# The opening stage of a hybrid GLA and pooling block: modulation columns, folds and early products by eighths of the features in place of quarters

## The chip, the cores and the metric

The kernel runs on one core of a Trainium2 chip. The metric is the device time of one execution in microseconds (us), the median over several runs. The core has five engines with instruction queues of their own: TensorE (PE, with its weight loads shown apart as PEld), VectorE (DVE), ScalarE (ACT), GpSimd (POOL) and SyncE (SP). SP issues nearly all DMAs here. Sixteen DMA engines move the bytes. Engines order themselves by semaphores, written out by hand in this kernel.

## The reference

One inference step of one transformer-like block, for 128 prompt tokens and 512 sample tokens (640 in all) of width 2048. What matters here is its beginning:

```python
xp = layer_norm(x_prompt, ln_in_g, ln_in_b)              # xs alike
mod_ctx = silu(c_ctx) @ w_ada + b_ada                    # 2048 x 12288; mod_lat alike from c
sh1, sc1, g1, sh2, sc2, g2 = split(mod, 6)
h = x * (1 + sc1) + sh1                                  # per feature, one pair for each token group
z = h @ w_in                                             # 33 units of 128 output columns
...                                                      # GLA scans, pooling, w_out, layer norm
gate, up = split(h2 @ w_gu, 2)                           # h2 = x * (1 + sc2) + sh2
y = layer_norm(ALPHA * x + g2 * ((silu(gate) * up) @ w_down))
```

All of it is float32. The kernel splits each operand of the big products into a high part and a rest and adds three products (high x high, high x rest, rest x high).

## The kernel before, in words

The features (2048) lie on the partitions in 16 blocks of 128, numbered k; the 640 tokens are the free dimension, in two halves of 320. Before any product of `w_in` can run on a block k, that block of h must be there, and for it the scale and shift of its 128 features: two sections of 2048 columns of `w_ada`, 33.5 MB in all. This opening stage, the prologue, does the following.

- **Loads.** SP issues, in one order written by hand: two small tables, the five token tiles of x (1 MB each), the steps of `w_ada`, and between them the first `w_in` units (1 MB each). `load_first` loads step i: 512 rows of the contraction by 512 columns, 1 MB in rows of 2 KB. `FIRST_SLOT` names its buffer; a buffer is loaded again once the step that used it before has been multiplied (`first_used`). Buffer 9 is the first half of `raw_w` and waits for three finished weight splits. `UNIT_AFTER` says after which step a unit is loaded; `load_unit(u)` for u of 2 or more waits until `split_done` reaches u - 1.
- **Input layer norm.** DVE takes the moments of an x tile, ACT its root and the normalisation, PE turns it (`turn_x`), DVE and ACT copy the result out to `xT`. PE's queue has these turns between the first four steps.
- **Modulation.** `ada_step` multiplies one step: four column groups of the array at once. Four steps fill one bank with a row of 512 columns (scale: bank 6, shift: bank 7). ACT copies the row out (`first_row`), PE turns it into columns and sums the groups (`first_cols`), DVE adds the bias (`add_bias`). Each quarter of the features needs eight steps, four for the scale and four for the shift.
- **Fold and split.** DVE folds the gain and bias of the layer norm into scale and shift (`fold_norm`, four small instructions in a chain). ACT applies them to a block of `xT` (two instructions, for the two token groups), DVE casts the high part and subtracts for the rest (`split_tile`, semaphore `h_split`). Blocks alternate between two temporary buffers. Weight units are split likewise (`split_in` on ACT, `split_rest` on DVE).
- **Early products.** The first three units (`EARLY`) are multiplied piece by piece while modulation is still running: `main_part(n, b)` is unit n by the four blocks of quarter b, 24 matmuls. They stand in PE's queue behind steps 2, 5 and 7 of the next quarter. After step 31 the last quarter of all three units follows.
- **Afterwards.** ACT copies unit 0 out (`evac(0)`), then splits unit 3, whose buffer unit 0 has left (`split_in(3)`, wait on `unit_used`), DVE makes its rest, and PE starts unit 3. From here a schedule of 33 units, `w_out`, the FFN and the down product follows; SP's next loads wait for the 16th block and then for `unit_used` of 3, and POOL's first work behind its first memset waits for the 16th block too.

PE runs its queue strictly in order: a wait in front of an early product holds the steps behind it.

Of the kernel before, what the change touches and what calls it, by code (L numbers as in the profile page):

```python
# [166 lines left out]
FIRST_STEPS = 32  # L167
# [158 lines left out]
def backbone(nc, x_all, state_gla, w_ada, w_in_b, wa2, w_pool_l, w_out, w_gu_b, w_down, consts,  # L326
# [91 lines left out]

    def first_slot(i):

        if i < 8:
            at = 2 * D + STEP * i
            return x_raw[:, at:at + STEP].rearrange("p (k c) -> p k c", k=4)
        src = lo(S_X, STEP) if i == 8 else raw_w[:, 0, :]
        return src.rearrange("p (k c) -> p k c", k=4)
# [9 lines left out]
    FIRST_USES = [[i for i in range(FIRST_STEPS) if FIRST_SLOT[i] == n] for n in range(N_FIRST)]  # L435
# [83 lines left out]
    first_in = [sem(f"first_in{i}") for i in range(N_FIRST)]  # L519
# [139 lines left out]
    def _(sp):  # L659
# [46 lines left out]
        sp.wait_ge(first_used, FIRST_USES[9][-1] + 1)  # L706
# [258 lines left out]
    def _(act):  # L965
# [295 lines left out]
        act.wait_ge(folded, 5)  # L1261
# [108 lines left out]
    def _(dve):  # L1370
# [42 lines left out]
        def add_bias(i, q, dst, src, done):  # L1413

            bias = b_ada_col[:, i, 4 * q:4 * q + 4].unsqueeze(2).to_broadcast([P, 4, 2])
# [31 lines left out]
        for q in range(4):  # L1447
            for g in range(2):
                i = 2 * q + g
                section = SECTIONS[g][1]  # L1450
                if i == 3:
                    split_rest(2)
                dve.wait_ge(mod_turned, i + 1)
                add_bias(section, q, mod_col[:, section, 4 * q:4 * q + 4, :],
                         ps[:, 6 + g, 0:8].rearrange("p (k c) -> p k c", c=2), mod_cols)
            dve.wait_ge(mod_cols, 2 * q + 2)
            fold_norm(V_LNIN, 4 * q, 4)
            if q == 0:
                split_rest(0)
            for k in range(4 * q, 4 * q + 4):  # L1460
                dve.wait_ge(h_tmp, k + 1)
                split_tile(high[:, PRO_TMP + (k % 2) * T:PRO_TMP + (k % 2) * T + T], k, h_split)
            if q == 0:
                split_rest(1)
# [53 lines left out]
        for kind, a, b, uses in SCHEDULE:  # L1518
# [3 lines left out]
            elif kind == "adacol":  # L1522
# [5 lines left out]
                add_bias(2 + slot, q, mod_col[:, slot, 4 * q:4 * q + 4, :],  # L1528
# [234 lines left out]
        dve.wait_ge(folded, 5)  # L1763
# [261 lines left out]
    def _(pe):  # L2025
# [21 lines left out]
        def main_part(n, b):  # L2047

            part = KG_ORDER[b] if n == N_IN - 1 else b
            for half in range(2):  # L2050
                for k in range(4 * part, 4 * part + 4):
# [19 lines left out]
        def first_cols(i):  # L2071
# [3 lines left out]
            for k in range(4):  # L2075
# [5 lines left out]
        used = [0] * N_FIRST  # L2081
        for i in range(FIRST_STEPS):
            n = FIRST_SLOT[i]
            used[n] += 1
            q, m = i // 8, i % 4
            pe.wait_ge(first_in[n], 16 * used[n])
# [391 lines left out]
```

## Time and profile before

| | us |
|---|---|
| three runs | 2706.84, 2711.62, 2713.73 |
| median | 2711.62 |
| profiled execution, its own time | 2708.05 |
| profiled execution, span of the trace | 2706.2 |

| engine | busy us | share of the span |
|---|---|---|
| PE | 2637.0 | 97% |
| PEld | 2352.4 | 87% |
| DVE | 1443.2 | 53% |
| ACT | 897.4 | 33% |
| POOL | 639.6 | 24% |

The page divides the span into 40 slices of 67.7 us. PE is busy for 5 tenths in the first slice and for 9 or more in all others up to the last (7). Modulation and the early products lie in the first two slices. All times within the trace are counted from the start of the span.

### The profile page before, as it was taken

What the parts mean: (1) busy time and instruction counts of PE and PEld (TensorE: products, weight loads), DVE (VectorE), ACT (ScalarE), POOL (GpSimd) and SP (SyncE); (2) the same over time, 40 slices, a digit from 0 to 9 for tenths busy, and PEclk for the clock granted to TensorE, in tenths of its full rate; (3) what the DMA queues carried; (4) which work ended last, traced back from release to release, by engine and by line L of the source; (5) the groups of instructions that cost most, each with busy time, mean ns of one, the idle gap of its engine ahead of it and who ended that gap; (6) DMA issues with size and microseconds to landing.
All of it is one profiled execution on the core that took longest, in us unless ns stands there. A gap on an engine that the chain in (4) does not pass through costs nothing.

```text
span 2706.2 us, 37404 instructions
## 1 busy us (share of the span) xinstructions
PE 2637.0 (97%) x16040; PEld 2352.4 (87%) x16040; DVE 1443.2 (53%) x1681; ACT 897.4 (33%) x940; POOL 639.6 (24%) x217
## 2 busy tenths in 40 slices
PE   5999999999999999999999999999999999999997
PEld 3687878797988879999999999999999888888875
DVE  5323332346575458666555545555556444454578
ACT  4333333332311154333333333333333333333343
POOL 0000000000000001434443444344433333333440
PEclk8999999999999999999999999999999999999999
DMA  9775757422463142332233323322334645464576
GB/s 373 285 268 208 275 202 273 158 90 87 181 219 118 63 161 81 109 108 89 92 108 109 94 87 109 109 92 89 109 109 152 242 173 211 173 212 166 207 245 238
DMA packets 179384, 438.11 MB, mean 162 GB/s; under 512 B 9980, under 2 KB 25732, under 8 KB 173076
## 3 DMA queue, kind: packets, MB, share of 16 engines
q1 hardware_dynamic: 176916, 430.48, 46.0%
q10 hardware_dynamic: 2304, 5.24, 0.5%
q8 instruction: 127, 2.08, 0.3%
q14 instruction: 37, 0.30, 0.0%
HBM read 401.83 MB, written 33.85 MB: 161 GB/s over the span
## 4 chain that ended last, share of the span: by engine, by line
PE 79%; DVE 6%; DMA 5%; POOL 4%; ACT 2%; issue 2%; SPq 1%; POOLq 0%; ACTq 0%; DVEq 0%
PE ps L2310 10%; PE ps L2311 10%; PE ps L2312 10%; PE ps L2387 6%; PE ps L2389 6%; PE ps L2388 6%; PE ps L2063 5%; PE ps L2065 5%; PE ps L2064 5%; PE ps L2257 3%; PE ps L2043 3%; PE ps L2259 3%; PE ps L2258 3%; DMA raw_w<-w_gu_b 2%; PE ps L2104 2%
## 5 line engine op out<-in xcount | busy, mean ns | idle before, releaser
L1670 DVE TENSOR_TENSOR w_lo<-raw_w,w_hi 128x1024 fp32r<-128x1024 f32 x264 | 348.2, 1320 | 299.8 <-ACT w_hi L1214 297.5
L1214 ACT ACTIVATE w_hi<-raw_w 128x1024 fp32r<-128x1024 f32 x264 | 270.2, 1054 | 610.5 <-POOL raw_w L954 370.5
L2310 PE MATMUL ps<-x_hi,w_hi 128*128 128x320 f32 x1408 | 436.2, 310 | 2.1 <-DVE x_lo L1750 1.4
L2312 PE MATMUL ps<-x_hi,w_lo 128*128 128x320 f32 x1408 | 435.1, 309 | 0.0
L2311 PE MATMUL ps<-x_lo,w_hi 128*128 128x320 f32 x1408 | 435.0, 309 | 0.0
L1805 DVE TENSOR_TENSOR x_lo<-low,x_hi 128x2560 fp32r<-128x2560 f32 (+2 forms) x55 | 223.6, 4065 | 261.3 <-ACT x_hi L1307 261.3
L945 POOL TENSOR_TENSOR low<-raw_w 128x1024 f32<-128x1024 f32 x41 | 101.2, 2469 | 1094.6 <-DMA raw_w<-w_gu_b 1027.5
L2387 PE MATMUL ps<-w_hi,x_hi 128*128 128x512 f32 x880 | 343.1, 390 | 3.3 <-DVE w_lo L1965 1.9
L2389 PE MATMUL ps<-w_hi,x_lo 128*128 128x512 f32 x880 | 342.4, 389 | 0.0
L2388 PE MATMUL ps<-w_lo,x_hi 128*128 128x512 f32 x880 | 342.4, 389 | 0.0
L2310 PE MATMUL ps<-low_r,w_hi 128*128 128x320 f32 x1072 | 332.0, 310 | 2.3 <-DVE w_lo L1670 1.5
L2312 PE MATMUL ps<-low_r,w_lo 128*128 128x320 f32 x1072 | 331.2, 309 | 0.0
L2311 PE MATMUL ps<-low_r,w_hi 128*128 128x320 f32 x1072 | 331.2, 309 | 0.0
L2063 PE MATMUL ps<-x_hi,w_hi 128*128 128x320 f32 x1024 | 324.4, 317 | 6.6 <-ACT low L1109 4.8
L2065 PE MATMUL ps<-x_hi,w_lo 128*128 128x320 f32 x1024 | 317.8, 310 | 0.0
L2064 PE MATMUL ps<-x_lo,w_hi 128*128 128x320 f32 x1024 | 317.7, 310 | 0.0
L960 POOL TENSOR_TENSOR w_lo<-raw_w,w_hi 128x2048 fp32r<-128x2048 f32 x44 | 203.9, 4633 | 355.5 <-ACT w_hi L1316 355.5
L2310 PEld LDWEIGHTS ps<-x_hi,w_hi 128*128 128x128 f32 x1408 | 264.3, 188 | 3.4 <-issue 1.6
L2311 PEld LDWEIGHTS ps<-x_lo,w_hi 128*128 128x128 f32 x1408 | 264.3, 188 | 0.0
L2312 PEld LDWEIGHTS ps<-x_hi,w_lo 128*128 128x128 f32 x1408 | 264.3, 188 | 0.0
L1381 DVE TENSOR_TENSOR w_lo<-raw_w,w_hi 128x2048 fp32r<-128x2048 f32 x48 | 110.0, 2291 | 259.0 <-ACT w_hi L981 258.8
L1316 ACT ACTIVATE w_hi<-raw_w 128x2048 fp32r<-128x2048 f32 x55 | 105.4, 1917 | 378.8 <-PE ps L2389 360.9
(239 smaller groups left out, 4358.0 us busy)
## 6 DMA issues: line engine op xcount, KB each, us to landing
raw_w<-w_gu_b SPq DMA_DIRECT2D x180, 512.0 KB, 5.7
low<-w_ada SPq DMA_DIRECT2D x68, 1024.0 KB, 6.9
raw_w<-w_down SPq DMA_DIRECT2D x55, 1024.0 KB, 5.1
low<-hidden_scratch SPq DMA_DIRECT2D x33, 1280.0 KB, 6.0
raw_w<-w_in_b SPq DMA_DIRECT2D x33, 1024.0 KB, 9.1
x_raw<-w_ada SPq DMA_DIRECT2D x25, 1024.0 KB, 15.4
raw_w<-w_out SPq DMA_DIRECT2D x16, 1024.0 KB, 5.2
hidden_scratch<-high SPq DMA_DIRECT2D x44, 320.0 KB, 5.9
```

The source lines that it names most:

```text
L1214: nc.scalar.activation(weight(0, w), src, ACT.Copy).then_inc(prod_hi, 1)
L1670: nc.vector.tensor_tensor(weight(1, n), src, weight(0, n).bitcast(F32), ALU.subtract).then_inc(prod_split, 1)
L1805: nc.vector.tensor_tensor(hid_slot(x_lo, j), hid_raw(j), hid_slot(x_hi, j).bitcast(F32), ALU.subtract).then_inc(hid_split, 1)
L2063: mm(out, wh, xh, start=first, stop=False)
L2064: mm(out, wh, xl, start=False, stop=False)
L2065: ins = mm(out, wl, xh, start=False, stop=last)
L2310: mm(out, wh, version(v, 0, k), start=first and k == 0, stop=False)
L2311: mm(out, wh, version(v, 1, k), start=False, stop=False)
L2312: ins = mm(out, wl, version(v, 0, k), start=False, stop=last and k == HK - 1)
L2387: mm(ps[:, (i + 7) % 8, :], xh, rh, start=begin, stop=False)
L2388: mm(ps[:, (i + 7) % 8, :], xh, rl, start=False, stop=False)
L2389: ins = mm(ps[:, (i + 7) % 8, :], xl, rh, start=False, stop=end)
```

## The change

A step becomes half as wide: 256 columns, 512 KB in rows of 1 KB, so 64 steps in place of 32. Eight steps now serve an eighth of the features, two blocks. Columns, bias, fold, ACT's affine pass, split and early products all go by two blocks (`early_part`, 12 matmuls). Each 1 MB buffer holds two steps; two more buffers are opened in blocks 0 to 6 of `xT`, free once seven blocks are split. Steps now count on 16 semaphores of their own, and step i is issued only once step i - 16 has been multiplied. `EARLY_PARTS` gives for each unit which eighths are multiplied behind steps 2, 5 and 7 of which eighth. ACT and DVE split weight units 0, 1 and 2 after the blocks of eighths 0, 1 and 2; before, they split unit 0 ahead of the blocks, unit 1 after the first quarter and unit 2 in the second. Unit 4 is loaded once step 63 has been multiplied.

```diff
-FIRST_STEPS = 32
+FIRST_STEPS = 64
...
-UNIT_AFTER = {7: 0, 8: 1, 11: 2, 31: 3}
+UNIT_AFTER = {7: 0, 11: 1, 15: 2, 63: 3}
...
-FIRST_SLOT = (0, 1, 2, 3, 4, 5, 6, 7, 0, 1, 2, 5, 6, 7, 8, 0, 1, 2, 9, 6, 7, 8, 1, 6, 2, 9, 7, 8, 2, 9, 7, 8)
-N_FIRST = 10
+FIRST_SLOT = (0, 1, 2, 3, 4, 5, 6, 7, 0, 1, 2, 5, 6, 7, 8, 0, 1, 2, 9, 6, 7, 8, 2, 9, 7, 8, 2, 9, 10, 11, 8, 9)
+N_FIRST = 12
+FIRST_IN_FLIGHT = 16
+EIGHTHS = 8
+EARLY_PARTS = ({e: (e - 1,) for e in range(1, 8)},
+               {2: (0, 1), 3: (2,), 4: (3,), 5: (4,), 6: (5,), 7: (6,)},
+               {3: (0, 1), 4: (2, 3), 5: (4,), 6: (5,), 7: (6,)})
...
+    def first_place(i):
+
+        return 2 * FIRST_SLOT[i // 2] + i % 2
...
         def load_first(i):
 
-            n = FIRST_SLOT[i]
+            n = first_place(i)
             before = [j for j in FIRST_USES[n] if j < i]
+            if i >= FIRST_IN_FLIGHT:
+                sp.wait_ge(first_used, i - FIRST_IN_FLIGHT + 1)
             if before:
                 sp.wait_ge(first_used, before[-1] + 1)
-            elif n == 8:
+            elif n // 2 == 8:
                 sp.wait_ge(turned, 4)
-            elif n == 9:
+            elif n // 2 == 9:
                 sp.wait_ge(split_done, 3)
-            group, part = SECTIONS[i // 4 % 2][0], i // 8
-            sp.dma_start(first_slot(n), w_ada_v[group, part, i % 4]).then_inc(first_in[n], 16)
+            elif n // 2 > 9:
+                sp.wait_ge(h_split, 7)
+            group, e = SECTIONS[i // 4 % 2][0], i // 8
+            c = 256 * (e % 2)
+            sp.dma_start(first_slot(i), w_ada_v[group, e // 2, i % 4][:, :, c:c + 256]
+                         ).then_inc(first_in[i % FIRST_IN_FLIGHT], 16)
...
-        sp.wait_ge(first_used, FIRST_USES[9][-1] + 1)
+        sp.wait_ge(first_used, max(FIRST_USES[18] + FIRST_USES[19]) + 1)
         load_unit(4, w_in_b[4])
...
-            nc.scalar.activation(high[:, at:at + 512], ps[:, 6 + i % 2, :], ACT.Copy).then_inc(mod_rows, 1)
+            nc.scalar.activation(high[:, at:at + 256], ps[:, 6 + i % 2, 0:256], ACT.Copy).then_inc(mod_rows, 1)
...
-        first_row(0)
-        first_row(1)
-        split_in(0)
-        for q in range(4):
-            if q:
-                first_row(2 * q)
-                if q == 1:
-                    split_in(2)
-                first_row(2 * q + 1)
-            for k in range(4 * q, 4 * q + 4):
+        for e in range(EIGHTHS):
+            first_row(2 * e)
+            first_row(2 * e + 1)
+            for k in range(2 * e, 2 * e + 2):
                 tmp = high[:, PRO_TMP + (k % 2) * T:PRO_TMP + (k % 2) * T + T]
-                if k % 4 == 0:
-                    act.wait_ge(folded, k // 4 + 1)
+                if k % 2 == 0:
+                    act.wait_ge(folded, e + 1)
...
-            if q == 0:
-                split_in(1)
+            if e < EARLY:
+                split_in(e)
...
-        for q in range(4):
+        for e in range(EIGHTHS):
...
+                dve.wait_ge(mod_turned, 2 * e + g + 1)
+                add_bias(section, 2 * e, 2, mod_col[:, section, 2 * e:2 * e + 2, :],
+                         ps[:, 6 + g, 0:4].rearrange("p (k c) -> p k c", c=2), mod_cols)
+            dve.wait_ge(mod_cols, 2 * e + 2)
+            fold_norm(V_LNIN, 2 * e, 2)
+            for k in range(2 * e, 2 * e + 2):
                 dve.wait_ge(h_tmp, k + 1)
                 split_tile(high[:, PRO_TMP + (k % 2) * T:PRO_TMP + (k % 2) * T + T], k, h_split)
-            if q == 0:
-                split_rest(1)
+            if e < EARLY:
+                split_rest(e)
...
-            for k in range(4):
+            for k in range(2):
                 c = PRO_ROW + 512 * (i % 2) + k * P
...
+        def early_part(n, e):
+
+            for half in range(2):
+                for k in range(2 * e, 2 * e + 2):
...
+                    if half == 0:
+                        pe.wait_ge(h_split, k + 1)
+                    mm(out, wh, xh, start=k == 0, stop=False)
+                    mm(out, wh, xl, start=False, stop=False)
+                    ins = mm(out, wl, xh, start=False, stop=k == KT - 1)
+            if e == EIGHTHS - 1:
+                ins.then_inc(unit_used, 1)
...
             if i % 8 == 4:
                 first_cols(i // 4 - 1)
             elif i % 8 == 7:
                 first_cols(i // 4)
-            if q and i % 8 in (2, 5, 7):
+            if i % 8 in (2, 5, 7):
                 u = (2, 5, 7).index(i % 8)
-                pe.wait_ge(split_done, u + 1)
-                main_part(u, q - 1)
+                for part in EARLY_PARTS[u].get(e, ()):
+                    pe.wait_ge(split_done, u + 1)
+                    early_part(u, part)
         for u in range(EARLY):
-            main_part(u, 3)
+            early_part(u, EIGHTHS - 1)
```

## Rows read from the trace of the kernel before

**Rows 1.** The page, its span.

```profile
span 2706.2 us, 37404 instructions
```

**Rows 2.** Windows of 10 us: busy us of PE, PEld, DVE, ACT, POOL, then PEclk, DMA share, GB/s.

```profile
50.00:60.00 10.00, 6.68 (x27) 3.29 (x28) 6.14 (x8) 4.20 (x5) 0.00 (x0) 0.50 1.04 395
...
80.00:90.00 10.00, 9.65 (x74) 6.54 (x67) 1.83 (x4) 0.90 (x2) 0.00 (x0) 1.00 1.03 371
...
120.00:130.00 10.00, 8.24 (x52) 7.24 (x51) 5.09 (x8) 5.66 (x10) 1.10 (x3) 1.00 0.00 0
130.00:140.00 10.00, 10.00 (x70) 10.00 (x69) 4.58 (x2) 3.83 (x6) 0.00 (x0) 1.00 0.39 129
```

**Rows 3.** Timeline of PE at the end of the prologue: start us, duration us, instruction.

```profile
114.29 1.06 PE L2043 MATMUL ps<-x_raw,perm 128*32 128x512 f32 x8
115.17 1.04 PE L2043 MATMUL ps<-low,perm 128*32 128x512 f32 x8
116.93 1.05 PE L2077 MATMUL ps<-perm,high 128*128 128x2 f32 x8 [0.72 <-ACT high L1006]
117.85 0.40 PE L2063 MATMUL ps<-x_hi,low_r 128*128 128x320 f32 x1
...
121.56 0.42 PE L2063 MATMUL ps<-x_hi,w_hi 128*128 128x320 f32 x1
...
122.83 0.41 PE L2063 MATMUL ps<-x_hi,w_hi 128*128 128x320 f32 x1 [0.54 <-DVE x_lo L1438]
...
134.79 0.31 PE L2063 MATMUL ps<-x_hi,w_hi 128*128 128x320 f32 x1
```

**Rows 4.** Timeline of DVE at the end of the prologue.

```profile
120.68 0.83 DVE L1438 TENSOR_TENSOR x_lo<-high,x_hi 128x640 fp32r<-128x640 f32 x1
...
121.94 0.83 DVE L1438 TENSOR_TENSOR x_lo<-high,x_hi 128x640 fp32r<-128x640 f32 x1
...
130.53 2.29 DVE L1381 TENSOR_TENSOR w_lo<-raw_w,w_hi 128x2048 fp32r<-128x2048 f32 x1 [5.14 <-ACT w_hi L981]
```

**Rows 5.** Timeline of ACT at the end of the prologue.

```profile
116.28 0.60 ACT L1006 ACTIVATE high<-ps 128x512 f32<-128x512 f32 x1 [8.63 <-PE ps L2043]
...
120.41 0.80 ACT L1038 ACTIVATE high<-low,perm 128x512 f32<-128x512 f32 x1
...
127.95 0.75 ACT L1071 ACTIVATE low<-ps 32x320 f32<-32x320 f32 x2 [3.95 <-PE ps L2065]
128.60 1.90 ACT L981 ACTIVATE w_hi<-raw_w 128x2048 fp32r<-128x2048 f32 x1
```

**Rows 6.** SP's DMA queue in 70:80, 116:120 and 2640:2650: packets, MB, share of 16 engines.

```profile
q1 hardware_dynamic: 1952, 3.87, 104.4%
...
q1 hardware_dynamic: 141, 0.97, 58.8%
...
q1 hardware_dynamic: 2086, 3.12, 91.7%
```

**Rows 7.** Timeline of PE later on: a group of 20 small matmuls.

```profile
175.91 0.80 PE L2158 MATMUL ps<-low 128*64 128x64 f32 x20
```

**Rows 8.** Timelines of PE, ACT and SP early in the prologue.

```profile
14.53 1.94 PE L2043 MATMUL ps<-x_raw,perm 128*32 128x512 f32 x8 [14.53 <-DMA x_raw<-w_ada]
16.40 3.68 PE L2037 MATMUL ps<-perm,low 128*128 128x128 f32 x16
...
44.47 1.05 PE L2077 MATMUL ps<-perm,high 128*128 128x2 f32 x8 [0.72 <-ACT high L1006]
...
57.55 0.47 PE L2064 MATMUL ps<-x_lo,w_hi 128*128 128x320 f32 x1
57.82 0.47 PE L2065 MATMUL ps<-x_hi,w_lo 128*128 128x320 f32 x1
...
12.34 2.09 ACT L997 ACTIVATE low<-low,perm 128x2048 f32<-128x2048 f32 x1 [0.43 <-DVE perm L1410]
...
48.84 0.34 SPq L683 DMA_DIRECT2D raw_w<-w_in_b  x1
```

More of the change, by code:

```diff
@@ L416, in mv @@
         return cols(C_MV + 4 * t + i, n)
+    def first_place(i):
+        return 2 * FIRST_SLOT[i // 2] + i % 2
     def first_slot(i):
[L421 to L424, printed above, removed]
+        n, at = FIRST_SLOT[i // 2], STEP // 2 * (i % 2)
+        if n < 8:
+            src = x_raw[:, 2 * D + STEP * n + at:2 * D + STEP * n + at + STEP // 2]
+        elif n == 9:
+            src = raw_w[:, 0, at:at + STEP // 2]
+        else:
+            src = lo((S_X if n == 8 else STEP * (n - 10)) + at, STEP // 2)
         return src.rearrange("p (k c) -> p k c", k=4)
@@ L433, in ring_slot @@
         return lo(L_PA + (i % RING) * STEP, STEP).rearrange("p (k c) -> p k c", k=4)
-    FIRST_USES = [[i for i in range(FIRST_STEPS) if FIRST_SLOT[i] == n] for n in range(N_FIRST)]
+    FIRST_USES = [[i for i in range(FIRST_STEPS) if first_place(i) == n] for n in range(2 * N_FIRST)]
     xT = lo(S_XT, 10240).rearrange("p (k c) -> p k c", k=KT)
@@ L518, in backbone @@
     turned_out_a = sem("turned_out_a")
-    first_in = [sem(f"first_in{i}") for i in range(N_FIRST)]
+    first_in = [sem(f"first_in{i}") for i in range(FIRST_IN_FLIGHT)]
     first_used = sem("first_used")
@@ L1260, in _ @@
         ln1_root(3)
-        act.wait_ge(folded, 5)
+        act.wait_ge(folded, EIGHTHS + 1)
         for a in range(4):
@@ L1411, in ln_in, with add_bias @@
                                            ALU.mult).then_inc(in_scale, 1)
-        def add_bias(i, q, dst, src, done):
-            bias = b_ada_col[:, i, 4 * q:4 * q + 4].unsqueeze(2).to_broadcast([P, 4, 2])
+        def add_bias(i, k, n, dst, src, done):
+            bias = b_ada_col[:, i, k:k + n].unsqueeze(2).to_broadcast([P, n, 2])
             nc.vector.tensor_tensor(dst, src, bias, ALU.add).then_inc(done, 1)
@@ L1446, in _ @@
         evac_turned(TT - 1)
-        for q in range(4):
+        for e in range(EIGHTHS):
             for g in range(2):
-                i = 2 * q + g
                 section = SECTIONS[g][1]
[L1451 to L1457, printed above, removed]
-            if q == 0:
-                split_rest(0)
-            for k in range(4 * q, 4 * q + 4):
+                dve.wait_ge(mod_turned, 2 * e + g + 1)
[4 more added lines that the diff above has]
+            for k in range(2 * e, 2 * e + 2):
                 dve.wait_ge(h_tmp, k + 1)
                 split_tile(high[:, PRO_TMP + (k % 2) * T:PRO_TMP + (k % 2) * T + T], k, h_split)
-            if q == 0:
-                split_rest(1)
+            if e < EARLY:
+                split_rest(e)
         def pool_tile(grp, j):
@@ L1527, in _ @@
                 q = a % 4
[L1528 removed]
+                add_bias(2 + slot, 4 * q, 4, mod_col[:, slot, 4 * q:4 * q + 4, :],
                          pair(x, 8).rearrange("p (k c) -> p k c", c=2), drained[x])
@@ L1761, in hidden_plain @@
                                     ps[:, PLAIN_BANK[g][1], 0:HALF], ALU.mult).then_inc(gated, 1)
-        dve.wait_ge(folded, 5)
+        dve.wait_ge(folded, EIGHTHS + 1)
         first, second = slice(0, VER // 2), slice(VER // 2, VER)
@@ L2038, in turn_x, with ada_step @@
                 ins.then_inc(turned, 1)
-        def ada_step(bank, tile, m, done):
+        def ada_step(bank, tile, m, done, n=512):
             for j in range(4):
-                ins = mm(ps[32 * j:32 * j + 32, bank, :], cond_pad[:, 4 * m + j, :], tile[:, j, :],
+                ins = mm(ps[32 * j:32 * j + 32, bank, 0:n], cond_pad[:, 4 * m + j, :], tile[:, j, :],
                          start=m == 0, stop=m == 3)
@@ L2057, in main_part @@
                     xl = x_lo[:, k, half * HALF:(half + 1) * HALF]
-                    if n < EARLY and half == 0:
-                        pe.wait_ge(h_split, k + 1)
-                    if n >= EARLY and first:
+                    if first:
                         i = 2 * (n - EARLY) + half
@@ L2079, in first_cols @@
             ins.then_inc(mod_turned, 1)
-        used = [0] * N_FIRST
+        def early_part(n, e):
+            for half in range(2):
+                for k in range(2 * e, 2 * e + 2):
+                    wh = w_part(0, n)[:, k * P:(k + 1) * P]
+                    wl = w_part(1, n)[:, k * P:(k + 1) * P]
+                    out = ps[:, main_bank(n, half), 0:HALF]
+                    xh = x_hi[:, k, half * HALF:(half + 1) * HALF]
+                    xl = x_lo[:, k, half * HALF:(half + 1) * HALF]
+                    if half == 0:
[5 more added lines that the diff above has]
+                ins.then_inc(unit_used, 1)
         for i in range(FIRST_STEPS):
[L2083 to L2086, printed above, removed]
+            e, m = i // 8, i % 4
+            pe.wait_ge(first_in[i % FIRST_IN_FLIGHT], 16 * (i // FIRST_IN_FLIGHT + 1))
             if m == 0 and i >= 8:
                 pe.wait_ge(mod_cols, i // 4 - 1)
-            ada_step(6 + i // 4 % 2, first_slot(n), m, first_used)
+            ada_step(6 + i // 4 % 2, first_slot(i), m, first_used, 256)
             for t in TURN_AFTER.get(i, ()):
```

## Prediction

> **What bounds the kernel now.** The page comes first [rows 1]: one execution of 2706.2 us, its own time 2708.05, which lies 3.6 us under the median 2711.62; I sum differences, so they apply to either. The windows come next [rows 2]. From 130 us on PE is busy for 10.00 of every 10 us, so whatever moves the first matmul of unit 3 moves the end by as much. Before that DMA is the scarce thing: 1.03 to 1.04 of its share until the loads are through, then 0.00 in 120:130. The timelines of PE, DVE and ACT around the last step give the chain behind it [rows 3, 4, 5]. Step 31 starts at 115.17, its columns at 116.93, PE then has unit 2's third quarter to do until 121.56, waits for a block or two, and reaches unit 3 at 134.79. All my times for the changed kernel are the start of the turn into shift columns of eighth e, called t(e); before, the last such turn is at 116.93, and unit 3 follows 17.86 us behind it.
>
> **What the tail gains.** Behind t(7) only two blocks are left.
> - The turn has 4 matmuls in place of 8: 117.85 - 116.93 = 0.92, so 0.46, and the chain after it comes 0.46 earlier. The first block was split at 120.68 + 0.83 = 121.51, 4.58 after the turn, the second at 122.77, 5.84 after [rows 3, 4]. Now they come at t + 4.1 and t + 5.4. The bias and fold instructions shrink from 8 to 4 columns, which I price at nothing (they are chains of tiny instructions).
> - A matmul of 320 columns costs 3.71 / 24 = 0.147 with its share of a gap (117.85 to 121.56) [rows 3]. Unit 0 has three matmuls on the first block, waits for the second, and has nine more: 5.43 + 1.32 = t + 6.75. Units 1 and 2 take 24 x 0.147 = 3.5: t + 10.3.
> - But unit 3's weights are late now. ACT copies unit 0 out 0.2 after its end (t + 6.95), takes 0.65, casts unit 3 in 1.93, DVE takes 2.29 [rows 4, 5]: t + 11.9. Before, this was ready at 132.82 and PE came at 134.79, so it was covered by 2 us; now PE stands 1.6 us at unit 3. The tail is 11.9 in place of 17.86: **5.96 us gained**.
>
> **What an eighth costs.** The order of PE's queue makes a loop: turn, unit 2's part, steps 0 to 2, then unit 0's part of the blocks just turned, and all later steps behind it.
> - Unit 0's part waits for the second block (t + 5.4), ends at t + 6.75; with 0.1 for the change of kind of matmul step 3 starts at t + 6.85. Before, this part came 24 matmuls' worth and three whole steps later, and the wait was covered.
> - A whole step takes 115.17 - 114.29 = 0.88, of which 0.86 is one; half the columns, 0.43. From a step's start to its turn was 116.93 - 115.17 = 1.76, with ACT's row copy at 0.60; now 1.76 - 0.43 - 0.25 (256 columns; ACT's copy of 320 is 0.75 / 2 or so) = 1.08 [rows 3, 5].
> - So: step 3 at t + 6.85, scale turn at 7.93, step 5 at 8.39, unit 1's part from 8.92 to 10.78, steps 6 and 7, next shift turn at 11.21 + 1.08 = **t + 12.3**.
> - Two parts of one unit in an eighth add 1.86 where they lie on this path (unit 1 in eighth 2) and 0.6 where they lie in the wait (unit 2 behind eighths 3 and 4: turn 0.46, two parts 3.7, steps 1.3 end at t + 5.5, then unit 0 needs 12 matmuls in full, t + 7.45).
>
> **What a half step costs in DMA.** With packets and bytes as two unknowns, 70:80 (1952 packets, 3.87 MB, 1.044 x 16 x 10 = 167.0 engine us) and 116:120 (141, 0.97 MB, 37.6) give 37.0 us for each MB and 12.2 ns for each packet [rows 6]. A row of 1 KB is then 50 ns, a step 512 x 50 / 16 / 1.04 = 1.54 us, where half an old step takes 1.36. The stretch 2640:2650, half of whose packets are 1 KB, comes to 141 by this and shows 146.7, so the price may be 4% low, and below it is bounded by no cost (1.36). Eight steps take 12.3 us: as long as PE's loop. The page "DMA: Bandwidth & Descriptors" of the Trainium skill, section "Specifications", says that rows from 512 B up move at line rate; by it the stretch would stay at 1.36 and 10.9 for an eighth. The rows speak against it, but since PE's loop is 12.3 anyway, only a rival hangs on this.
>
> **The timeline.**
> - Start: step 0 brings 0.5 MB less and lands 1.3 earlier than 14.53, so PE waits for the first normalised tile (12.34 + 2.09 = 14.43) and turns it at 14.5, not 16.40; the chain of turns moves up by 1.9 [rows 8]. The old shift turn was at 44.47; four half steps and short turns bring t(0) to about 40.3.
> - Eighth 0: second block at 45.7. ACT splits unit 0 only behind both blocks (t + 3.83 to 46.05), DVE's rest is done at 48.4. PE, which comes to unit 0's part at 42, waits for it, and SP, which has unit 2 behind the same semaphore, stands until 48.4. By then 5.2 MB of x, 16 half steps and 2.1 MB of units are through, at about 46; DMA idles some 4 us and resumes near 50. PE does not feel it: step 18 lands at 57.2, and PE waits for blocks until 60.
> - PE's 12 matmuls from 48.45 run at the lower clock (57.82 - 57.55 = 0.27 each, PEclk 0.50 in 50:60) [rows 2, 8]: 3.2 us. Steps 11 to 15 and two turns: t(1) = 55.9.
> - t(2) = 55.9 + 12.3 + 1.9 = 70.1; t(3) = 82.4; t(4) = 82.4 + 12.9 = 95.3; t(5) = 108.2; t(6) = 120.5; **t(7) = 132.8**.
> - DMA beside it: unit 2 lands at 52.6, step 63 at 52.6 + 48 x 1.54 = 126.5. Buffers do not stop it: the new ones (step 36 waits for unit 2's split at 78.2, with the queue full to 83.4), the 16 in flight, and reuse (step 48 issued at 100.3, needed at 101.9) all fit. Unit 3 is issued at about 121 and there by 129; unit 4, now behind step 63, lands near 138 and is split near 145. SP's later loads and POOL's memset hang on the 16th block and come with it.
>
> Unit 3 starts at 132.8 + 11.9 = 144.7, against 134.79: +9.9. PE idles for 2.3 us ahead of unit 0's part in eighths 2 and 3, after thin work; the old trace has the clock at 0.50 in 50:60 after waits of this kind [rows 2]. The lower clock costs 0.27 - 0.147 on each matmul, so about 2 us if some 16 run under it; I take one in two for one place: +1. The sum is **+10.9 us**: 2722.5, say 2723 (2719 for an execution like the profiled one).
>
> How fast small matmuls can be issued bounds the half step: eight in 0.43 is 54 ns each. The later group of 20 takes 0.80 us, 40 ns each [rows 7], so I keep 0.43. The Trainium skill's "TensorE: Matmul & The Clock Gate", section "Wait — 56ns, not 53.3ns?", gives 62 ns to a matmul whose decoding is done by the sequencer's code; by that a half step would be 0.50 and the sum 1 to 2 us more. This row shows less than 62.
>
> **The rivals.**
> - *DMA sets the pace.* If blocks are ready sooner than I think, the end follows step 63: 126.5 + 1.1 + 11.9 = 139.5, +4.7, 2716. For it: both loops are 12.3. Against: my chain is 5 us behind the loads by the end.
> - *The shorter tail wins* (the other side). The fold wait holds PE less and 1 KB rows cost nothing, as the page cited has it: step 63 lands at 52.6 + 48 x 1.36 = 117.9, the end at 130.9, -3.9, 2708; at most -7.8 (5.96 and the 1.8 by which PE took step 31 late). It decides once t(7) is under 134.79 - 11.9 = 122.9, that is a loop of (122.9 - 55.9 - 3.1) / 6 = 10.7 us. Against: the second block alone is at t + 5.4, and the steps behind it take as long again.
> - *Half steps do not halve.* At the whole step's 0.86, four on the path add 1.7 for each of six eighths, +10 more; with the clock low through eighths 2 and 3, +4. 2730 or so. Against: the four column groups stream side by side, so columns should set it.
>
> **How the numbers follow.** Forecast 0.63 (its own range 2715 to 2731, from the clock and from 0.2 to 0.3 us in each eighth), DMA 0.14, shorter tail 0.12, slow steps 0.11. 0.3%, 8.1 us, is about what can be told from no change here. Slower takes 0.55 of the forecast and the slow steps: 0.66. Within: 0.08, 0.14 and 0.09: 0.31. Faster by 8.1 is beyond even the bound of the second rival but for errors: 0.03. The range takes in half of each outer rival: 2709 to 2733.
>
> **What would show it.** PE's timeline: shift turns 12.3 us apart, with a wait on `x_lo` in front of every unit 0 part; one ahead of unit 3 on `w_lo`, 1.6 us. DMA share near 0 around 46 to 50, then about 340 GB/s (0.524 MB in 1.54 us); PE not waiting for steps in the last eighths. Unit 3 at 144 to 146. If turns come 11 us apart, or a 1 KB packet takes no more than half of a 2 KB one, I am wrong towards the second rival; if PE waits for DMA at steps 6 and 7, towards the first; if the x8 groups last over 0.6, towards the third.

## The result, and the profile after

The changed kernel takes 2725.99 us (median of 4 runs, 2724.05 to 2727.85); the kernel before took 2710.63 on the same chips (four runs, one more than stood in the table of before). The ratio is 1.0061 [1.0045, 1.0077]: slower by 15.4 us. The prediction had +10.9, 2723 us, and gave slower a chance of 0.66. The profiled execution took 2724.05 for a span of 2722.2, 16.0 above the span of before [rows 1].

Windows of 10 us after the change (PE, PEld, DVE, ACT, POOL busy with their counts, PEclk, DMA share, GB/s); two of them answer to [rows 2]:

```profile
30.00:40.00 10.00, 6.36 (x48) 4.50 (x48) 4.60 (x10) 6.36 (x8) 0.00 (x0) 0.83 1.06 368
40.00:50.00 10.00, 4.08 (x56) 2.40 (x56) 5.22 (x11) 4.47 (x6) 0.00 (x0) 0.98 0.64 206
50.00:60.00 10.00, 8.92 (x76) 6.11 (x76) 1.26 (x6) 0.77 (x2) 0.00 (x0) 0.68 0.88 292
80.00:90.00 10.00, 9.50 (x76) 6.64 (x76) 3.15 (x7) 0.80 (x3) 0.00 (x0) 0.83 1.09 348
100.00:110.00 10.00, 9.50 (x94) 7.25 (x97) 3.29 (x9) 2.68 (x5) 0.00 (x0) 1.00 0.56 180
```

Two things are to be seen: the hole in the loads in 40:50, which was predicted, and a second one in 100:110, which was not; and the share of 1.09 where loads run at only 348 GB/s. After the first step, at 13.45, PE does not wait for a load once up to unit 3.

PE's timeline after (start, duration, instruction, idle before), with the lines that answer to [rows 3] and [rows 8]. The lines on `perm,high` with x4 are the turns into columns; those at 42.59, 115.11, 127.81 and 140.53 turn shift rows:

```profile
31.58 2.81 PE L2044 MATMUL ps<-perm,x_raw 128*128 128x128 f32 x16 [2.72 <-ACT x_raw L1015]
...
42.59 0.61 PE L2082 MATMUL ps<-perm,high 128*128 128x2 f32 x4 [0.50 <-ACT high L1024]
...
50.58 0.63 PE L2097 MATMUL ps<-x_hi,w_hi 128*128 128x320 f32 x1 [5.95 <-DVE w_lo L1393]
...
62.95 0.38 PE L2097 MATMUL ps<-x_hi,w_hi 128*128 128x320 f32 x1 [2.21 <-DVE x_lo L1450]
...
115.11 0.61 PE L2082 MATMUL ps<-perm,high 128*128 128x2 f32 x4 [0.50 <-ACT high L1024]
115.57 0.40 PE L2097 MATMUL ps<-x_hi,low_r 128*128 128x320 f32 x1
...
119.36 0.38 PE L2097 MATMUL ps<-x_hi,w_hi 128*128 128x320 f32 x1 [0.34 <-DVE x_lo L1450]
...
120.53 0.41 PE L2097 MATMUL ps<-x_hi,w_hi 128*128 128x320 f32 x1 [0.49 <-DVE x_lo L1450]
...
122.04 0.64 PE L2050 MATMUL ps<-low,perm 128*32 128x256 f32 x8
122.49 0.61 PE L2050 MATMUL ps<-x_raw,perm 128*32 128x256 f32 x8
123.18 0.61 PE L2082 MATMUL ps<-perm,high 128*128 128x2 f32 x4
...
126.24 1.07 PE L2050 MATMUL ps<-raw_w,perm 128*32 128x256 f32 x16
127.81 0.61 PE L2082 MATMUL ps<-perm,high 128*128 128x2 f32 x4 [0.50 <-ACT high L1024]
...
140.53 0.61 PE L2082 MATMUL ps<-perm,high 128*128 128x2 f32 x4 [0.50 <-ACT high L1024]
...
144.69 0.42 PE L2097 MATMUL ps<-x_hi,w_hi 128*128 128x320 f32 x1 [1.68 <-DVE x_lo L1450]
...
152.70 0.39 PE L2068 MATMUL ps<-x_hi,w_hi 128*128 128x320 f32 x1 [1.65 <-DVE w_lo L1393]
```

All eight shift turns lie at 42.59, 58.70, 74.31, 88.45, 101.77, 115.11, 127.81 and 140.53. Before, they were at 44.47, 73.23, 94.88 and 116.93, one for each quarter, so the last two quarters took 10.8 and 11.0 for half a quarter; now an eighth takes 16.1, 15.6, 14.1, 13.3, 13.3, 12.7 and 12.7. Unit 3 starts at 152.70 against 134.79 [rows 3], +17.9, of which 16.0 are left at the end.

What the 17.9 are made of is told by two windows, from the first step to unit 3. Before:

```profile
14.00:134.79 120.79, 100.23 (x688) 68.48 (x689) 50.23 (x97) 48.99 (x68) 1.10 (x3) 0.94 0.89 335
```

After:

```profile
14.00:152.70 138.70, 108.63 (x944) 78.76 (x937) 53.79 (x122) 50.50 (x77) 1.10 (x3) 0.93 0.88 291
```

PE is busy for 8.4 us more with the same products, and idle for 30.1 in place of 20.6, 9.5 more. About half of the loss is waiting, the other half is work that takes longer. The low clock may have a share in both, but a stretch of each kernel at a clock of 1.00 shows the same. Before, from the third shift turn to the fourth, a quarter's work:

```profile
94.88:116.93 22.05, 20.59 (x152) 14.09 (x152) 6.02 (x14) 5.89 (x10) 0.00 (x0) 1.00 1.01 375
```

After, the eighth that starts with the turn at 115.11:

```profile
115.11:127.81 12.70, 11.29 (x108) 7.92 (x108) 3.45 (x10) 3.06 (x6) 0.00 (x0) 1.00 1.09 348
```

Half a quarter keeps PE busy for 10.3 us and idle for 0.7; an eighth keeps it busy for 11.3 and idle for 1.4.

SP's queue in 70:80 after, to be held against the first of [rows 6] (packets, MB, share of 16 engines):

```profile
q1 hardware_dynamic: 3471, 3.46, 108.6%
```

That is 1.086 x 160 / 3471 = 50 ns for a packet of 1 KB, as worked out beforehand.

### The profile page after: what moved, and what is told of

Its sections match the earlier page's. It is cut to its first block, busy times and chain, and to the rows that moved or that the text cites. A ratio compares the mean times of both kernels' runs of the same rounds, so it can differ in the third digit from the quotient of the medians.

```text
span 2722.2 us, 38068 instructions
## 1 busy us (share of the span) xinstructions
PE 2646.5 (97%) x16296; PEld 2365.0 (87%) x16296; DVE 1407.3 (52%) x1705; ACT 899.2 (33%) x948; POOL 647.9 (24%) x217
## 4 chain that ended last, share of the span: by engine, by line
PE 88%; DVE 5%; ACT 3%; DMA 2%; issue 1%; POOL 1%; SPq 0%; ACTq 0%; DVEq 0%; POOLq 0%
PE ps L2330 12%; PE ps L2332 12%; PE ps L2331 12%; PE ps L2407 6%; PE ps L2409 6%; PE ps L2408 6%; PE ps L2068 5%; PE ps L2070 5%; PE ps L2069 5%; PE ps L2050 3%; PE ps L2277 3%; PE ps L2279 2%; PE ps L2278 2%; PE ps L2124 2%; DMA raw_w<-w_down 1%
## 5 line engine op out<-in xcount | busy, mean ns | idle before, releaser
L1677 DVE TENSOR_TENSOR w_lo<-raw_w,w_hi 128x1024 fp32r<-128x1024 f32 x264 | 327.0, 1240 | 296.5 <-ACT w_hi L1226 293.4
L2330 PE MATMUL ps<-x_hi,w_hi 128*128 128x320 f32 x1408 | 435.7, 309 | 1.7 <-DVE x_lo L1757 0.8
L2332 PE MATMUL ps<-x_hi,w_lo 128*128 128x320 f32 x1408 | 435.1, 309 | 0.0
L2331 PE MATMUL ps<-x_lo,w_hi 128*128 128x320 f32 x1408 | 435.0, 309 | 0.0
L963 POOL TENSOR_TENSOR low<-raw_w 128x1024 f32<-128x1024 f32 x41 | 107.0, 2610 | 1084.5 <-DMA raw_w<-w_gu_b 1031.3
L2068 PE MATMUL ps<-x_hi,w_hi 128*128 128x320 f32 x960 | 302.7, 315 | 6.5 <-ACT low L1121 4.8
L2070 PE MATMUL ps<-x_hi,w_lo 128*128 128x320 f32 x960 | 297.2, 310 | 0.0
L2069 PE MATMUL ps<-x_lo,w_hi 128*128 128x320 f32 x960 | 297.1, 310 | 0.0
```

The lines of the kernel that those rows point to most:

```text
L1677: nc.vector.tensor_tensor(weight(1, n), src, weight(0, n).bitcast(F32), ALU.subtract).then_inc(prod_split, 1)
L2068: mm(out, wh, xh, start=first, stop=False)
L2069: mm(out, wh, xl, start=False, stop=False)
L2070: ins = mm(out, wl, xh, start=False, stop=last)
L2330: mm(out, wh, version(v, 0, k), start=first and k == 0, stop=False)
L2331: mm(out, wh, version(v, 1, k), start=False, stop=False)
```

## The experiments

Theory A is the prediction's: PE's queue sets the pace, as unit 0's early part waits for the fold of the blocks just turned, and loads lie beside it. Theory B: the loads set it, by their small rows or by the holes in 40:50 and 100:110. Theory C, formed from the profile after: the low clock of the thin first 60 us. Experiments 1 to 4 and then 5 to 8 ran beside runs of the kernel before with medians 2707.18 and 2708.11; 9 to 12 beside 2706.04. Ratios are to the kernel before on the same chip.

### 1. Unit 0's part behind step 5

```diff
-            if i % 8 in (2, 5, 7):
-                u = (2, 5, 7).index(i % 8)
+            for u in {5: (0, 1), 7: (2,)}.get(i % 8, ()):
                 for part in EARLY_PARTS[u].get(e, ()):
```

> The changed kernel with one move: unit 0's early part no longer stands behind step 2 of an eighth, in front of the blocks it has to wait for, but behind step 5, ahead of unit 1's. If the wait for the second block inside PE's queue makes the loop of 12.7 to 14 us, it is gone: shift turns come at the pace of the loads, eight half steps or 12.1 us, and the last one is at 128 to 131 in place of 140.5. Time 2714 to 2717. If the loads or the row size set the pace, nothing moves: 2726 as the changed kernel, last turn at 140.

Measured: 2727.15 us, ratio 1.0070 [1.0058, 1.0083], shift turns at 42.97, 56.89, 75.78, 89.64, 102.64, 115.64, 126.88 and 138.12, unit 3 at 150.29. PE's timeline shows both halves of the answer:

```profile
58.81 0.64 PE L2050 MATMUL ps<-x_raw,perm 128*32 128x256 f32 x8 [1.32 <-DMA x_raw<-w_ada]
...
81.70 0.61 PE L2082 MATMUL ps<-perm,high 128*128 128x2 f32 x4 [3.02 <-ACT high L1024]
...
126.88 0.61 PE L2082 MATMUL ps<-perm,high 128*128 128x2 f32 x4 [0.50 <-ACT high L1024]
...
138.12 0.61 PE L2082 MATMUL ps<-perm,high 128*128 128x2 f32 x4 [0.50 <-ACT high L1024]
```

The last loops take 11.24 in place of 12.7. Not all of these 1.46 us were waiting: PE's idle time in a loop falls from 1.41 to 0.58, by the 0.34 and 0.49 that it stood in front of the two blocks, and its busy time from 11.29 to 10.66, since unit 0's part now runs on into unit 1's, without a change of the kind of matmul at either end of its old place. But PE, no longer held, now catches up with the loads: it waits for steps from 58 to 65, the clock stands at 0.51 in 60:70, and the eighth that follows takes 18.9. A third wait comes out as well: the scale turn stands 3.02 behind ACT's row copy, which has a weight split ahead of it. The expectation was missed, in the last turn (138.12 for 128 to 131) and in the time: a wait taken away alone uncovered two others.

### 2. Unit 2 loaded after step 23

```diff
-UNIT_AFTER = {7: 0, 11: 1, 15: 2, 63: 3}
+UNIT_AFTER = {7: 0, 11: 1, 23: 2, 63: 3}
```

> The changed kernel with unit 2 loaded behind step 23 in place of step 15, so that SP does not stand at its semaphore and the DMA engines do not idle from 46 to 51.5. If PE's own queue sets the pace the end does not move: 2726 within 1.5. If the loads set it, the 5 us of idle DMA come back: 2721.

Measured: 2726.05 us, ratio 1.0072 [1.0059, 1.0086], last turn at 141.19. The window in which the loads had stood:

```profile
40.00:50.00 10.00, 4.82 (x66) 2.55 (x64) 4.14 (x11) 5.49 (x9) 0.00 (x0) 1.00 1.09 349
```

The share is 1.09 in place of 0.64, and PE has nothing from it, as expected if PE's queue sets the pace. Theory B's first hole does not matter as long as PE waits elsewhere.

### 3. Unit 0 split ahead of the first two blocks

ACT's `split_in(0)` moves to just behind `first_row(1)` and DVE's `split_rest(0)` to just behind the first `fold_norm`, as before the change:

```diff
             first_row(2 * e + 1)
+            if e == 0:
+                split_in(0)
...
-            if e < EARLY:
+            if 0 < e < EARLY:
                 split_in(e)
```

> The changed kernel with unit 0 split ahead of the first two blocks on ACT and DVE, as in the kernel before. The first part of unit 0 waits for the later of both, which moves from 50.6 to about 49, and SP is released near 47. If PE's queue sets the pace: 1.3 to 2 us less, 2724. If the idle DMA sets it: 4 to 5 less, 2721.

Measured: 2724.73 us, ratio 1.0062 [1.0050, 1.0074]. Unit 0's first part stands 3.44 us and starts at 49.54, where it stood 5.95 and started at 50.58; from a first turn 1.5 later the first interval falls from 16.1 to 13.2, and the last turn is at 137.92 (-2.6). The time, expected at 2724, cannot be told from that of the changed kernel.

### 4. The kernel before, with rows of 1 KB

Each step of the old kernel comes by two DMAs of 256 columns; its work is otherwise the same.

```diff
-            sp.dma_start(first_slot(n), w_ada_v[group, part, i % 4]).then_inc(first_in[n], 16)
+            for c in (0, 256):
+                sp.dma_start(first_slot(n)[:, :, c:c + 256],
+                             w_ada_v[group, part, i % 4][:, :, c:c + 256]).then_inc(first_in[n], 16)
...
-            pe.wait_ge(first_in[n], 16 * used[n])
+            pe.wait_ge(first_in[n], 32 * used[n])
```

> The kernel before, with each of its 32 steps loaded by two DMAs of 256 columns, so rows of 1 KB, and nothing else changed. By the price from the rows (1 KB packets 50 ns in place of 43 for each KB) the loads end 12 us later, at 125 in place of 113, PE had 1.8 us of slack there: 10 us more, 2721. If rows from 512 B up move at line rate: no change, 2711.

Measured: 2716.83 us, ratio 1.0031 [1.0019, 1.0043], +9.7. PE's timeline, the end of the prologue, with waits on the loads where [rows 3] has none:

```profile
117.94 1.06 PE L2045 MATMUL ps<-raw_w,perm 128*32 128x512 f32 x8 [0.97 <-DMA raw_w<-w_ada]
...
124.02 1.07 PE L2045 MATMUL ps<-low,perm 128*32 128x512 f32 x8 [0.30 <-DMA low<-w_ada]
125.80 1.05 PE L2079 MATMUL ps<-perm,high 128*128 128x2 f32 x8 [0.72 <-ACT high L1008]
```

The last turn is 8.9 later than before. A row of 1 KB takes 50 ns, half of a row of 2 KB 43 (1.044 x 160 / 1952 / 2) [rows 6]. With 16384 packets more, at 12.2 ns each over 16 engines, loading takes 12.5 us longer, and where the loads are the bound most of it shows. The edit also doubles the number of DMAs; that it is the rows that count follows from experiment 6, which keeps 64 DMAs, gives them longer rows and runs at 408 GB/s. It leaves the question whether the changed kernel pays it too.

### 5. The three together

Edits 1, 2 and 3 in one kernel.

> The changed kernel with the three edits of the first runs together: unit 0's part behind step 5, unit 2 loaded behind step 23, unit 0 split ahead of the first blocks. Singly they moved the last shift turn from 140.5 to 138.1, 141.2 and 137.9. If what costs is PE's own queue from the start of the prologue on (waits for the first split, thin work at the low clock, then eighths of 11.2 to 13 us of matmuls), they add up: shift turns at 55, 68, 80, 93, 106, 117 and 128, unit 3 at 140 to 142, 10 to 12 us under the changed kernel (2714 to 2716), still 5 over the kernel before. If each only hands the wait on to another, the last turn stays above 136 and the time within 4 of 2726.

Measured: 2722.39 us, ratio 1.0053 [1.0041, 1.0066]; turns at 43.83, 53.57, 67.66, 81.52, 94.52, 107.50, 118.74 and 129.99.

```profile
118.74 0.61 PE L2086 MATMUL ps<-perm,high 128*128 128x2 f32 x4 [0.50 <-ACT high L1024]
...
129.99 0.61 PE L2086 MATMUL ps<-perm,high 128*128 128x2 f32 x4 [0.50 <-ACT high L1024]
...
142.16 0.39 PE L2072 MATMUL ps<-x_hi,w_hi 128*128 128x320 f32 x1 [1.65 <-DVE w_lo L1395]
```

Unit 3 comes 10.5 earlier than in the changed kernel. Of this 3.6 lie in the last four loops (13.00, 12.98, 11.24 and 11.25 for 13.3, 13.3, 12.7 and 12.7) and 8.2 in the first three, less 1.2 for a later first turn. Singly the edits gave 2.4, -0.7 and 2.6 in unit 3's start. That they work only together, since each removes the wait that hid another's, fits the traces of experiments 1 and 5, but the sum of 4.3 against 10.5 does not secure it: in two executions of one program the last turn differs by 3.6 to 4.0 us (experiments 9 and 10). Even so the loop never falls under 11.24, and unit 3 is 7.4 later than before. What the 11.24 consist of, the last loop tells:

```profile
118.74:129.99 11.25, 10.67 (x109) 8.03 (x109) 3.45 (x10) 3.06 (x6) 0.00 (x0) 1.00 0.83 284
```

PE is busy for 10.67 of it, and 0.50 is the wait for ACT's copy of the row in front of the shift turn, which no experiment takes away.

The expectation was right in the turns (to 2 us) and in unit 3, and missed in the time: 2722 where it had 2714 to 2716. The section on the prediction comes back to the difference.

### 6. The changed kernel with rows of 4 KB

`w_ada` is laid out in memory in the order of the steps, so each of the 128 partitions reads 4 KB in one piece. Loads and work keep their order and sizes.

```diff
-            c = 256 * (e % 2)
-            sp.dma_start(first_slot(i), w_ada_v[group, e // 2, i % 4][:, :, c:c + 256]
-                         ).then_inc(first_in[i % FIRST_IN_FLIGHT], 16)
+            sp.dma_start(first_slot(i), w_first[group, e, i % 4]).then_inc(first_in[i % FIRST_IN_FLIGHT], 16)
```

> The changed kernel with w_ada laid out step by step in memory, so that a half step is 128 rows of 4 KB in place of 512 of 1 KB; instructions of all engines the same. The loads should run at some 400 GB/s in place of 347. If PE's queue sets the pace the last shift turn stays at 140 to 141 and the time at 2726 within 2. If the row size of 1 KB is what made the change slower, 9 to 12 less: 2714 to 2717.

Measured: 2727.6 us, ratio 1.0075 [1.0061, 1.0089], last turn at 141.23, unit 3 at 153.41.

```profile
40.00:50.00 10.00, 4.87 (x66) 2.55 (x64) 4.09 (x11) 5.55 (x9) 0.00 (x0) 1.00 0.24 97
...
70.00:80.00 10.00, 7.24 (x71) 5.31 (x70) 2.89 (x9) 3.84 (x6) 0.00 (x0) 1.00 1.03 408
```

408 GB/s in place of 347, and nothing comes of it. This is the clearest verdict: in the changed kernel the loads are not what sets the time. (The layout covers all of `w_ada`, so the sections that are loaded later have longer rows too; the last turn and unit 3 lie before them.)

### 7. The kernel before with rows of 8 KB

The same layout for the old steps of 512 columns, again for all of `w_ada`, the later sections included.

```diff
-    w_ada_v = w_ada.rearrange("(m k p) (g q c) -> g q m p k c", p=P, k=4, g=6, q=4)
+    w_ada_v = w_ada.rearrange("(g q m p k c) -> g q m p k c", g=6, q=4, m=4, p=P, k=4)
```

> The kernel before with w_ada laid out step by step, rows of 8 KB in place of 2 KB. The loads of the prologue end 8 us sooner. If the loads alone bound the prologue before, 8 us less. PE was 92 to 98% busy from 62 us on, so by the theory that PE's work fills the prologue it gains only its waits for steps, 3 to 5 us: 2703 to 2706 where the kernel before has 2708.

Measured: 2703.18 us, ratio 0.9986 [0.9977, 0.9995], about 3.8 us under the kernel before; last turn at 111.70, 5.2 earlier.

```profile
70.00:80.00 10.00, 10.00 (x74) 7.77 (x74) 5.85 (x13) 4.69 (x8) 0.00 (x0) 1.00 1.01 419
```

PE is now busy for all of this window, at 419 GB/s. Had the loads alone bound the prologue, the expectation had 8 us less; what came is its other branch, PE's waits for steps. After the first step these were 7.6 us before (1.76, 3.77, 0.76, 0.21, 0.35 and 0.75) and are 4.2 now (3.60 and 0.56); 0.8 us more come from an earlier first turn. So the kernel before was bound by its loads for a few us and by PE's own work for the rest, and larger rows pay for these few. Of the 5.2 us, 4.6 are left at the first product of `w_out` and 0.6 at the first of the FFN, since PE then waits 4.4 us for DVE's `x_lo` among the products of `w_out`, where before it did not; the span ends 3.2 shorter. How much of the gain in time is due to the prologue and how much to the longer rows of the later sections was not separated. The gain is under the 0.3% that the prediction took as what can be told, but with 11 runs its interval does not contain 1.

### 8. Fillers for the clock

Products of the identity into unused columns of a bank, in PE's idle places: 8 ahead of each turn of x but the first, 30 ahead of unit 0's first part and 11 ahead of its second and third.

```diff
+        def fill(n, bank):
+
+            for _ in range(n):
+                mm(ps[:, bank, 320:512], ident, perm[:, 0:192], start=True, stop=True)
...
+                if t:
+                    fill(8, 1)
                 turn_x(t)
...
+                if i % 8 == 2:
+                    fill({1: 30, 2: 11, 3: 11}.get(e, 0), 1 if e == 1 else 5)
```

> The changed kernel with idle stretches of PE filled by matmuls whose result nobody reads (8 ahead of each turn of an x tile but the first, 30 ahead of unit 0's first part, 11 ahead of its second and third), into banks that are free there; the outputs stay the reference's. If the low clock cost what I think (turns of x at 2.8 in place of 1.97, the first part at 0.27 a matmul, and falls near 62 and 80), PEclk stays at 1.00 from 20 us on and the last shift turn comes 4 to 5 us sooner, at 136: 2722. If the clock cost nothing that was not idle anyway, 140.5 or later, and 2726.

Measured: 2725.45 us, ratio 1.0067 [1.0055, 1.0080]; turns at 41.82, 59.17, 74.20, 87.47, then as in the changed kernel to 139.55.

```profile
30.00:40.00 10.00, 9.44 (x79) 7.85 (x81) 4.28 (x10) 5.85 (x8) 0.00 (x0) 1.00 1.06 372
...
60.00:70.00 10.00, 9.93 (x93) 7.99 (x86) 5.58 (x10) 4.47 (x6) 0.00 (x0) 1.00 1.09 348
```

The clock stays at 1.00 from 20 to 140, and the last turn comes 1.0 earlier. The 30 fillers took longer than the wait that they filled (17.35 for the first interval, was 16.1); eighths 2 and 3 gained 15.6 - 15.0 and 14.1 - 13.3, 1.4 in all, and the start 0.8. Theory C is worth 2.2 us of prologue, less than expected, and the fillers give 1.2 of it back. In this execution none of it reaches unit 3, since the clock fell in the tail instead, where it had not in the changed kernel: from 144.97 on eleven matmuls run at 0.27 each, and unit 3 starts at 152.91, 0.2 later than without fillers.

```profile
144.97 0.63 PE L2097 MATMUL ps<-x_hi,w_hi 128*128 128x320 f32 x1 [0.56 <-DVE x_lo L1450]
...
152.91 0.38 PE L2068 MATMUL ps<-x_hi,w_hi 128*128 128x320 f32 x1 [1.37 <-DVE w_lo L1393]
```

### 9 and 10. The changed kernel and the three edits again, on one chip

> The changed kernel once more, so that it stands on one chip beside the one with all three edits. 15 to 16 above the kernel before; last shift turn near 140.5.

> The three edits together once more. In the first trace the last shift turn came at 130.0, 10.5 ahead of the changed kernel's, but the time was 14 above the kernel before, where 5 to 8 follow from the prologue. If the saving in the prologue reaches the end, this is 7 to 10 under the changed kernel on the same chip. If later stages take it back, the turn is again at 130 and the time only 1 to 4 under it, and the traces show in which stage.

Measured: 2728.9 us, ratio 1.0082 [1.0069, 1.0096], against 2720.55, ratio 1.0052 [1.0040, 1.0064]: 8.35 apart on the same chip, within the 7 to 10 that were expected, and the intervals do not touch. So the three edits' gain is real; at unit 3 it is 10.15 (156.31 and 146.16). Two other expectations were missed: the changed kernel is 22.9 above the kernel before here, not 15 to 16, and the last turn of the three edits is at 133.99, not at 130. The changed kernel's own prologue differs from one execution to the next: its last turn was at 144.13 here and at 140.53 in the first profile. The window shows what goes with it:

```profile
30.00:40.00 10.00, 7.80 (x39) 6.59 (x40) 3.00 (x6) 4.11 (x6) 0.00 (x0) 0.50 1.06 370
```

The clock stood at 0.50 where it was 0.83 in the first profile. Of the 3.6 us, 3.2 are there at the first shift turn already (45.76 for 42.59).

### 11. The three edits with rows of 4 KB

Edits 1, 2, 3 and 6.

> The three edits together with rows of 4 KB. With the waits gone, do the loads matter? In the trace with rows of 1 KB PE waited once for a step in the later eighths (0.75 us). If PE's matmuls fill the loop (11.24 us), the last turn comes at 129 to 130, no more than 1 us sooner; if the loads now set the pace, 4 or more sooner.

Measured: 2721.45 us, ratio 1.0056 [1.0044, 1.0068], beside 2720.55 for the rows of 1 KB; turns at 46.89, 56.65, 72.27, 87.63, 100.63, 113.61, 124.86 and 136.08. The last turn was expected at 129 to 130; it came 6 later, and longer rows are no reason for that: PE's clock stood at 0.50 in 40:50 of this execution and did not stay at 1.00 before 90. The last loops are 13.0, 13.0, 11.2 and 11.2, as with rows of 1 KB: with the fold wait and the loads both gone, PE's queue takes 11.24, of which 10.67 is work and 0.50 the wait for the row copy.

### 12. The kernel before with rows of 8 KB, and one part earlier

Experiment 7, and unit 0's part of quarter 0 one step earlier (behind step 9 in place of 10).

```diff
-            if q and i % 8 in (2, 5, 7):
-                u = (2, 5, 7).index(i % 8)
+            if i == 9 or q and i != 10 and i % 8 in (2, 5, 7):
+                u = (2, 5, 7).index(i % 8) if i != 9 else 0
```

> The kernel before with rows of 8 KB, and unit 0's first part in front of the third step of the second quarter in place of behind it. It would start at about 50.5 with its first block, in time that PE now spends waiting at the low clock, and all later work of the prologue follows 1.5 to 2.5 sooner: last turn at 109.5 to 110.5 in place of 111.7, time 2701 to 2703. If the blocks or the clock give nothing, 111.7 and 2704.

Measured: 2702.54 us, ratio 0.9987 [0.9978, 0.9995]; last turn at 112.40.

```profile
60.10 1.06 PE L2043 MATMUL ps<-x_raw,perm 128*32 128x512 f32 x8 [1.22 <-DMA x_raw<-w_ada]
...
112.40 1.05 PE L2077 MATMUL ps<-perm,high 128*128 128x2 f32 x8 [0.72 <-ACT high L1006]
```

The time is within the expected range, the last turn is not: 0.7 later than in experiment 7, where 1.2 to 2.2 earlier was expected. PE now waits 1.22 for a step at 60.10 and 0.43 at 62.58, where it did not in experiment 7: part of the wait moved to the loads. There is no gain that can be told from experiment 7's. The two kernels with rows of 8 KB are the best of the study.

## Why the prediction held, and where it was off

The sign and the range were right, and so was the mechanism in the main: a shorter tail, paid for in each loop of PE's queue and not by the loads. Some luck is in the number: unit 3 came 17.9 late where 10.9, with the term for the clock, was forecast, 7.0 off; the median is only 4.5 off, because 2.5 us of it do not show at the end, which the prediction did not foresee. Step by step:

- **The tail.** Forecast 11.9 from the last turn to unit 3, measured 152.70 - 140.53 = 12.17 (17.86 before). Second block after the turn: forecast 5.4, measured 145.95 - 140.53 = 5.42. Unit 3 stands 1.65 on its weights; forecast 1.6.
- **The loop.** Forecast 12.3, measured 12.70. In the eighth of 115.11 the second block comes at +5.42 (5.4), step 3 at +6.93 (6.85), the scale turn at +8.07 (7.93), steps 6 and 7 at +11.13 (10.78). Where PE goes from one kind of matmul to another about 0.1 us passes (step 3 starts 0.24 after the last matmul of unit 0's part, where 0.147 is the pace within it), five times in this stretch, and I had taken them once. Over six loops that is 2.4 us.
- **What the loop is made of.** Here the emphasis was wrong. I told it as a fold wait. The trace has 0.83 us of waiting for blocks in a loop of 12.70, and experiment 1, which takes 1.46 away, takes 0.63 of it from PE's busy time. What is left is 11.24, more than the 10.8 and 11.0 that half a quarter took with its waits. PE's work alone is 11.3 for an eighth where half a quarter has 10.3 at the same clock; I had not compared these two. With every wait on a fold gone, and the early start that I had forecast, the last turn would be at 40.3 + 7 x 11.24 + 3 double parts of 1.76 = 124.3, and unit 3 12.17 later at 136.4: still behind 134.79. This estimate keeps the wait of 0.50 for ACT's row copy in each loop. Seven of them are 3.5 us, more than the 1.6 that are missing, so it is not shown that no version by eighths can come up with the kernel before.
- **The start.** t(0) forecast 40.3, measured 42.59: PE was to be ready for x early, but it began to turn x at 15.04, not at 14.5, and two turns of x ran in part at the lower clock (2.85 and 2.81 where experiment 8 has 1.91 to 1.97), with the clock at 0.83. t(1) - t(0): 16.1, forecast 15.6. The term for the clock was +1, at one place; it was at three (start, eighths 2 and 3), and with the two loops there came to 1.4 and 1.8 over the forecast, 0.4 in each of it from the changes of kind. This and the loop make the 7.7 by which the last turn is late (140.53 against 132.8). The step that was mis-sized is "I take one in two for one place: +1".
- **The loads.** 50 ns for a row of 1 KB and the hole from 46 to about 51 are as forecast; the share is 1.09 where I had taken 1.04, so a step takes 1.51 and not 1.54. "Buffers do not stop it" was wrong: SP waited for step 48's buffer until 106.69, since PE was later than I had it. PE felt nothing of it. The Trainium skill's "DMA: Bandwidth & Descriptors", section "Specifications", has rows from 512 B up at line rate; experiments 4 and 7 decide against it here, at 348, 387 [rows 6] and 419 GB/s for rows of 1, 2 and 8 KB.
- **Half steps.** Forecast 0.43, measured 122.49 - 122.04 = 0.45, 56 ns for each of eight matmuls. The Trainium skill's "TensorE: Matmul & The Clock Gate", section "Wait — 56ns, not 53.3ns?", has 62 ns for a matmul that the sequencer's code decodes; this trace does not show it.

The rivals: *DMA sets the pace* fell with experiment 6; its price was right for the kernel before (experiment 4, +9.7) and was covered in the changed one. *The shorter tail wins* needed a loop under 10.7; no version by eighths that was run came below 11.24. *Half steps do not halve* fell with the row above.

**Open.** Unit 3 moved by 17.9, the median by 15.4 and the span by 16.0; in experiment 5 unit 3 is 7.4 late, its span 10.2 over and its median 14.3. Part of that lies in one place. The stretch from the first product of `w_out` to the FFN takes 238.1 or 238.2 us in the kernel before, in both executions of the changed kernel and in experiments 4, 6 and 8; 240.0 in experiment 1 and in both executions of the three edits; 240.7, 240.8 and 243.3 in experiments 3, 11 and 2; 242.1 and 242.3 in experiments 7 and 12. The two programs that were profiled twice have the same figure both times, so it seems to go with the program and not with chance. In experiment 5 the granted clock is 0.59 in 982:992, near its end, and in experiment 2 it is 0.50 in 995:1005, where the changed kernel has 0.83; in experiments 7 and 12 it is 1.00 near the end, and PE waits 4.4 and 4.9 for `x_lo`. Why a shift of the prologue decides on either was not tested. The rest, the other 2 us that the changed kernel gets back and the 4 us between span and median in experiment 5, stays open; a part of it may be the difference between executions.

## What to carry to other kernels

Finer pieces shorten what comes after the last piece (5.7 us here), but are paid once per piece: count the changes of kind, the row copies and the waits in one loop of the busiest queue, and compare both its work and the waits that will stay with what the old loop takes. Here its work alone, 11.3 us for 10.3, was enough to eat up the shorter tail over seven loops. When several waits lie side by side, taking away one can show the next; judge them by an experiment with all of them gone. And before transfers are cut into shorter rows, or where they are the bound, look at the time of a packet: laying the weights out so that a partition reads 8 KB in one piece was the only edit here that made the kernel faster, by 3.8 us. And follow a gain to the end: of 5.2 us in the prologue 0.6 were left at the FFN.

## What was not expected of the hardware

- The time of a DMA packet in this queue is told within 3% by 12.2 ns and 37.0 us for each MB from rows of 1 KB to rows of 8 KB; the windows 70:80 have 347, 387, 408 and 419 GB/s for 1, 2, 4 and 8 KB.
- The same program, run twice, had the granted clock at 0.83 or at 0.50 in 30:40, while PE turned tiles of x with waits between them, and its last turn at 140.53 or 144.13. The kernel with the three edits had its last turn at 129.99 and 133.99, with 0.73 and 0.83 there but 1.00 and 0.71 in 60:70. The three single edits of experiments 1 to 3 moved it by less.
- Filling the idle places kept the clock at 1.00 for 120 us and brought 1 us in the last turn. Then the clock fell in the tail, where nothing was filled, unit 3 came no sooner, and nothing can be told in the time.
